# Experts of a diffusion trunk: gate and up rows alternate with single banks of the down product

## The chip, the cores and the metric

The kernel runs on one core of one Trainium2 chip. The metric is the device time of one execution in microseconds. A second figure, the span, is the time from the first to the last instruction in one profiled execution.

## The reference

One layer of a trunk over 128 context tokens and 512 latent tokens of width 2048: adaLN modulation, a mixer (12 attention heads and 32 state-space groups), an output projection, and then a routed feed-forward part with 16 experts. Only the last is touched by the change. All of it is float32.

```python
def expert_choice_ffn(x, p):
    B, L, D = x.shape
    cap = CAPACITY_FACTOR * L // N_EXPERTS
    aff = jax.nn.softmax((x @ p['w_router']).astype(jnp.float32), axis=-1)
    g, idx = lax.top_k(jnp.swapaxes(aff, 1, 2), cap)
    bidx = jnp.arange(B)[:, None, None]
    xs = x[bidx, idx]
    h = (jax.nn.silu(jnp.einsum('becd,edf->becf', xs, p['w_gate']))
         * jnp.einsum('becd,edf->becf', xs, p['w_up']))
    y = jnp.einsum('becf,efd->becd', h, p['w_down']) * g[..., None].astype(x.dtype)
    return jnp.zeros_like(x).at[bidx, idx].add(y)
```

Each expert takes 64 latent and 16 context tokens (80 slots), has gate and up matrices of 2048x1024 and a down matrix of 1024x2048, 8 MB each, and adds its result to the output rows of its tokens.

## The kernel before, in words

The program is written engine by engine, and the order of each engine's instructions is the order in the source. Semaphores tie the engines together.

**Weights.** An expert's weights come in twelve pieces of 2 MB: pieces 0 to 7 hold in turn an eighth of what the gate and up products need (even ones gate, odd ones up: four of the sixteen 128-row blocks of the contraction), pieces 8 to 11 a quarter of down (two of its eight contraction blocks). SyncE (SP) issues them in the order 0, 1, 8, 2, 3, 9, 4, 5, 10, 6, 7, 11 into a ring of 8 slots (`w_ring`, which lies in the buffers `work` and `hT_`). Before each issue it waits until `s_used` says that the piece that was in the slot before has been multiplied. The profile puts that wait of SP at line 105 and the issue at line 690.

**TensorE.** `gate_up(s, j, r, rounds)` multiplies one gate or up piece (an "eighth"): 4 contraction blocks ("rows" here, one value of k each) of 8 blocks of hidden units in 2 halves, so 64 matmuls, 16 a row. The weights of the expert are the stationary side, 128x64, and the 80 tokens the moving side; the result lies in PSUM banks 0 to 2, summed over k. `down(e, s, k, r, rounds)` multiplies one contraction block of the down matrix of the expert before (an eighth of down): three banks (3, 4, 5), in each four matmuls side by side, each in its own strip of 32 columns of the array. There the hidden values are the stationary side (128x32 or 128x16) and 512 columns of weights the moving side.

**Order.** `expert(e, s, ...)` goes through nine steps j: in step j, the 64 matmuls of gate or up piece j of expert e (j below 8), then the 12 matmuls of down block j - 1 of expert e - 1 (j above 0), and in odd steps the transposes (`turn_four`, four matmuls at line 1187) of the next expert's tokens. At its start it waits for the hidden values of expert e - 1 (`s_hh`), which ScalarE (lines 1170, 1171) and VectorE (lines 2262, 2264) form from banks 0 to 2. In step 1 each bank of down waits for VectorE (lines 2276, 2280) to have read the result of the expert before it out of that bank (`s_ye`). The down block of an odd k, like every piece of gate and up, gives its slot back with its last matmul.

Expert 0 has gate and up alone, through `gate_up`. Fifteen calls of `expert` follow (e = 1 to 15), and at the end `last_down` (line 1795) does the down product of expert 15.

Of the kernel before, what the change touches and what calls it, by code (L numbers as in the profile page):

```python
# [15 lines left out]
KT = D // P  # L16
# [24 lines left out]
BANK = 512  # L41
# [6 lines left out]
START = 12  # L48
# [35 lines left out]
def trunk_step(nc, t, out):  # L84

    ctx = ExitStack()
    with ctx:
# [8 lines left out]
        def free_sem(name, start=START):  # L96


            s = sem(name)
            free.append((s, start))  # L100
            return s
# [13 lines left out]
        def bank(b, n=BANK, at=0):  # L115
            return PS[:, b * BANK + at:b * BANK + at + n]
# [197 lines left out]
        RING = RING_SLOTS  # L314
        w_ring = [work[:, i * 4096:(i + 1) * 4096] for i in (1, 6, 2, 3, 4, 5)] + [hT_[:, 6144:6144 + 4096], work[:, 0:4096]]
# [3 lines left out]
        xsT = [hT_[:, i * 1280:(i + 1) * 1280].rearrange("p (k s) -> p k s", k=KT) for i in range(2)]  # L319
        act_g = hT_[:, 2560:2560 + 8 * SLOTS]  # L320
        actT = [hT_[:, 3200 + i * 640:3840 + i * 640].rearrange("p (k s) -> p k s", k=8) for i in range(2)]
# [128 lines left out]
        s_used = free_sem("s_used")  # L450
        s_sg = sem("s_sg")
        s_hh = free_sem("s_hh")
        s_ye = free_sem("s_ye")
# [22 lines left out]
        ORDER = [0, 1, 8, 2, 3, 9, 4, 5, 10, 6, 7, 11]  # L476
# [708 lines left out]
        def _(pe):  # L1185
# [221 lines left out]
            for g in range(6 * TT):  # L1407
                m, at_ = (g - SSM_FIRST) // SSM_EACH, (g - SSM_FIRST) % SSM_EACH
# [192 lines left out]
            for k in range(1, 7):  # L1601
                tt = (k + 2) // 3
                first = 5 * ((k + 2) % 3)
# [79 lines left out]
            for tt in range(1, 4):  # L1683
                for s in range(5):
                    i = 5 * (tt - 1) + s
# [36 lines left out]
            def turn_four(e, s, b):  # L1722

                pe.wait_ge(s_xsev, 4 * e + b)
                for k in range(4 * b, 4 * b + 4):
                    last = turn(bank(7, P, (k - 4 * b) * P), xs[s][:, k * P:(k + 1) * P])
                last.then_inc(s_xsT, 1)

            def hidden_at(u, f):

                return bank(2 * u, SLOTS, f * SLOTS) if f < 6 else bank(1, SLOTS, (2 * u + f - 6) * SLOTS)

            def landed(r, rounds):
                pe.wait_ge(s_w[r % RING], 16 * (rounds + r // RING + 1))

            def gate_up(s, j, r, rounds):


                landed(r, rounds)
                u = j % 2  # L1740
                w = w_ring[r % RING].rearrange("p (k b m i) -> p k b i m", k=4, b=4, i=2)
                for k in range(4 * (j // 2), 4 * (j // 2) + 4):
                    for f in range(8):
                        opens = k == 0 and (f == 0 or (f == 6 and u == 0))
                        for h in range(2):
                            last = pe.matmul(hidden_at(u, f)[64 * h:64 * h + 64, :],  # L1746
                                             w[:, k % 4, f // 2, f % 2, 64 * h:64 * h + 64], xsT[s][:, k, :],
                                             start=opens, stop=(k == KT - 1), skip_group_check=True)
                last.then_inc(s_used, 1)

            def down(e, s, k, r, rounds):

                if k % 2 == 0:
                    landed(r, rounds)
                w = w_ring[r % RING].rearrange("p (k n) -> p k n", k=2)
                for c in range(3):
                    if k == 0:
                        pe.wait_ge(s_ye, START + 6 * (e - 1) + 2 * c + 2)
                    for g, first, n, col in ((0, 0, 32, c), (1, 32, 32, c), (2, 64, 16, c), (3, 32 * c, 32 if c < 2 else 16, 3)):
                        last = pe.matmul(bank(3 + c)[32 * g:32 * g + n, :], actT[s][:, k, first:first + n],  # L1760
                                         w[:, k % 2, col * BANK:(col + 1) * BANK], start=(k == 0), stop=(k == 7))
                if k % 2 == 1:
                    last.then_inc(s_used, 1)

            def expert(e, s, r0, rounds, tokens):

                pe.wait_ge(s_xsev, 4 * e + 4)
                pe.wait_ge(s_hh, START + 2 * e)
                for j in range(9):
                    if j < 8:  # L1770
                        gate_up(s, j, r0 + ORDER.index(j), rounds)
                    if j:
                        down(e - 1, 1 - s, j - 1, r0 + ORDER.index(8 + (j - 1) // 2), rounds)
                    if tokens is not None and j % 2 == 1:
                        if j == 1:
                            pe.wait_ge(s_gath[1 - s], tokens)
                        turn_four(e + 1, 1 - s, j // 2)
# [5 lines left out]
            for j in range(8):  # L1783
                gate_up(0, j, j, 0)
                if j % 2 == 1:
                    if j == 1:
                        pe.wait_ge(s_gath[1], 32)
                    turn_four(1, 1, j // 2)
            for e in range(1, EXPERTS):
                expert(e, e % 2, 12 * e - 4, 0, 32 * ((e + 1) // 2 + 1) if e + 1 < EXPERTS else None)  # L1790
# [503 lines left out]
        def _(pool):  # L2294
# [145 lines left out]
            def shifted(tt, b):  # L2440
                pool.wait_ge(s_scaled, SCALED + 4 * (tt - 3) + b + 1)
                rows, (_, shift) = turned_views(tt, b, shift2)
                TT_(rows, rows, shift, ALU.add).then_inc(s_h2, 1)
# [107 lines left out]
```

## Time and profile before

| | |
|---|---|
| median of 3 runs | 2412.14 us (2411.34 to 2412.56) |
| profiled execution, its own time | 2406.91 us |
| its span | 2405.1 us |
| mean granted TensorE clock over the span | 0.982 |
| the fifteen calls of `expert` (from 1404.20 to 2363.07 us of the span) | 958.87 us |
| busy: TensorE matmul / weight load | 2249.6 us (94%) / 1477.0 us (61%) |
| busy: VectorE / ScalarE / GpSimd | 716.9 / 480.9 / 621.2 us |
| data moved | 630.85 MB |

The profile names an instruction by its line, its engine, and output <- inputs. PE is TensorE's matmul and PEld its weight load. The trace shows every float32 matmul as two records of each kind where single records are counted (the timeline): the 64 matmuls of an eighth are x128 there, the four of a bank x8; the view by lines counts them once. Ends of matmuls are modelled, so starts are better to reckon with than ends. "issue" as a releaser means that the engine waited for nothing that the profile shows. The calls of `expert` are told apart by VectorE's instruction at line 2262, which runs once an expert.

### The profile page before, as it was taken

The numbers are of one execution on the slowest core, as the hardware profiler recorded it, in microseconds if no ns is written. First come the engines' busy times: TensorE is split into PE (matmuls) and PEld (weight loads), VectorE is DVE, ScalarE is ACT, GpSimd is POOL, SyncE is SP. The second block draws the span as 40 slices with busy tenths as digits, with TensorE's granted clock in tenths as the row PEclk, the third lists the DMA queues.
The fourth block names the chain that finished last, engine by engine and source line by source line (L and its number), as shares of the span: only waits on it lengthen the run. The fifth ranks groups of instructions, "written<-read, shape, count | busy, mean of one in ns | idle before, by whom it ended". The sixth has DMA issues, their size and how long they took to land.

```text
span 2405.1 us, 57415 instructions
## 1 busy us (share of the span) xinstructions
PE 2249.6 (94%) x25897; PEld 1477.0 (61%) x25897; DVE 716.9 (30%) x1172; ACT 480.9 (20%) x1020; POOL 621.2 (26%) x660
## 2 busy tenths in 40 slices
PE   5999999999999999999996589999999999999997
PEld 3468888656566565644443476667667666666663
DVE  4124442367767775311337000000000000000001
ACT  3011111356665654210024000000000000000000
POOL 0246771466766673000205100000000000000000
PEclk9999999999999999999998799999999999999999
DMA  9922222865565654240334989999999999999995
GB/s 370 365 84 60 86 55 70 228 201 163 188 220 166 201 193 145 98 157 27 143 122 175 334 333 395 408 409 409 409 414 410 416 414 410 410 408 402 407 405 184
DMA packets 184669, 630.85 MB, mean 262 GB/s; under 512 B 14618, under 2 KB 91204, under 8 KB 154020
## 3 DMA queue, kind: packets, MB, share of 16 engines
q1 hardware_dynamic: 165920, 587.11, 63.6%
q0 software_dynamic: 3328, 20.97, 3.3%
q10 hardware_dynamic: 15188, 19.19, 2.4%
q8 instruction: 203, 3.33, 0.6%
q14 instruction: 30, 0.25, 0.0%
HBM read 602.80 MB, written 24.44 MB: 261 GB/s over the span
## 4 chain that ended last, share of the span: by engine, by line
PE 69%; DMA 14%; DVE 6%; issue 4%; SPq 2%; ACT 2%; POOL 1%; ACTq 1%; DVEq 0%; POOLq 0%
PE PS L1746 19%; PE PS L1496 11%; PE PS L1587 10%; DMA work<-in_w_gate 9%; PE PS L1760 9%; PE PS L1310 8%; DMA hT_<-in_w_gate 3%; PE PS L1252 3%; PE PS L1187 3%; POOL work L2398 1%; DVE PS L2096 1%; PE PS L1214 1%; PE PS L1482 1%; DMA work<-in_w_ada 1%; DVE work L2055 1%
## 5 line engine op out<-in xcount | busy, mean ns | idle before, releaser
L1746 PEld LDWEIGHTS PS<-hT_,work 128*64 128x64 f32 x14336 | 512.0, 140 | 91.5 <-issue 71.2
L1746 PE MATMUL PS<-hT_,work 128*64 128x80 f32 x14336 | 530.8, 235 | 34.0 <-issue 21.0
L1496 PE MATMUL PS<-hT_,work 128*128 128x512 f32 (+1 forms) x1536 | 433.2, 434 | 0.0
L2398 POOL TENSOR_TENSOR work<-work 128x512 f32<-128x512 f32 x240 | 305.1, 1271 | 163.8 <-ACT work L1002 147.8
L1496 PEld LDWEIGHTS PS<-hT_,work 128*128 128x128 f32 x1536 | 226.5, 192 | 146.8 <-issue 146.7
L1760 PE MATMUL PS<-work,hT_ 128*32 128x512 f32 (+1 forms) x2544 | 298.6, 596 | 4.6 <-DMA work<-in_w_down 3.0
L2262 DVE TENSOR_TENSOR hT_<-PS,hT_ 128x480 f32<-128x480 f32 x16 | 10.5, 658 | 947.4 <-ACT hT_ L1170 947.4
L1587 PE MATMUL PS<-work,mixT_ 128*128 128x512 f32 x640 | 283.1, 598 | 0.0
L2480 POOL DMA_INDIRECT out_y<-mixT_,work x16 | 23.4, 1461 | 797.8 <-DVE mixT_ L2280 797.8
L1310 PE MATMUL PS<-work,hT_ 128*128 128x256 f32 x960 | 212.7, 381 | 0.7 <-DMA work<-in_w_in 0.7
L1164 ACT ACTIVATE hT_<-PS 128x256 f32<-128x256 f32 x64 | 24.5, 383 | 943.9 <-PE PS L1187 943.9
L1587 PEld LDWEIGHTS PS<-work,mixT_ 128*128 128x128 f32 x640 | 120.0, 191 | 142.0 <-issue 142.0
L1310 PEld LDWEIGHTS PS<-work,hT_ 128*128 128x128 f32 x960 | 180.6, 190 | 26.1 <-issue 1.2
L1002 ACT ACTIVATE work<-work,cT 128x512 f32<-128x512 f32 x256 | 172.7, 717 | 50.4 <-POOL work L2398 38.1
L1760 PEld LDWEIGHTS PS<-work,hT_ 128*32 128x32 f32 (+1 forms) x2544 | 70.4, 105 | 146.9 <-issue 134.8
L2096 DVE SCALAR_TENSOR_TENSOR PS<-work,cT,PS 128x512 f32<-128x512 f32 x208 | 155.9, 750 | 3.5
L1187 PE MATMUL PS<-consts,mixT_ 128*128 128x128 f32 (+2 forms) x403 | 62.2, 292 | 49.0 <-DMA mixT_<-h_rows,work 25.9
L1187 PEld LDWEIGHTS PS<-consts,mixT_ 128*128 128x128 f32 (+2 forms) x403 | 45.0, 153 | 101.1 <-issue 58.5
L1746 PEld LDWEIGHTS PS<-hT_ 128*64 128x64 f32 x2048 | 72.1, 139 | 14.5 <-issue 8.2
L1746 PE MATMUL PS<-hT_ 128*64 128x80 f32 x2048 | 75.0, 234 | 5.8 <-DMA hT_<-in_w_gate 4.6
L1252 PE MATMUL PS<-work,hT_ 128*128 128x512 f32 x160 | 73.7, 612 | 0.9 <-DVE hT_ L1920 0.9
L1187 PE MATMUL PS<-consts,work 128*128 128x128 f32 (+4 forms) x361 | 53.4, 267 | 19.2 <-DVE work L2249 8.0
(301 smaller groups left out, 1848.1 us busy)
## 6 DMA issues: line engine op xcount, KB each, us to landing
work<-in_w_up SPq DMA_DIRECT2D x57, 2048.0 KB, 27.3
work<-in_w_down SPq DMA_DIRECT2D x56, 2048.0 KB, 32.2
work<-in_w_gate SPq DMA_DIRECT2D x55, 2048.0 KB, 31.7
work<-in_w_ada SPq DMA_DIRECT2D x48, 2048.0 KB, 9.6
work<-in_w_in SPq DMA_DIRECT2D x80, 512.0 KB, 6.3
hT_<-in_w_gate SPq DMA_DIRECT2D x9, 2048.0 KB, 33.9
work<-in_w_out SPq DMA_DIRECT2D x4, 4096.0 KB, 13.7
hT_<-in_w_down SPq DMA_DIRECT2D x8, 2048.0 KB, 31.2
```

Source lines behind the costliest of these rows:

```text
L1002: act.activation(prod[i % 3] if k else acc_ctx[p % 3], late_ring[k // 8][:, k % 8, :], ACT.Identity, scale=cTv[:, 0, k:k + 1]).then_inc(s_ ...
L1164: act.activation(xsT[s][:, 4 * b:4 * b + 4, 0:CAP_L], rows[:, :, 0:P:2], ACT.Copy)
L1187: return pe.transpose(dst, src, ident[0:parts, 0:parts])
L1214: last = pe.matmul(bank(5 + part)[q:q + 32, :], cT_wide[:, k, :], w_ada_ring[n % ADA_RING][:, k % 8, :], start=(k < 4), stop=(k >= KT - 4))
L1252: last = pe.matmul(bank(tt), hT[:, k, tt * P:(tt + 1) * P], w_chunk[k // 2 % NW][:, BANK * (k % 2):BANK * (k % 2) + BANK], start=(k == 0), ...
L1310: last = pe.matmul(bank(g % 2, 256), hT[:, k, tt * P:(tt + 1) * P], w_chunk[chunk % NW][:, 256 * (k % 4):256 * (k % 4) + 256], start=(k == ...
L1496: last = pe.matmul(qk_bank(which)[:, (ctx_at if ctx_ else lat_at)[which]], w_chunk[chunk % NW][:, HD * (k % 8):HD * (k % 8) + HD], hT[:, k ...
L1587: last = pe.matmul(bank(tt), mix_at(k)[:, tt * P:(tt + 1) * P], w_out_ring[n % 2][:, k, :], start=(k == 0), stop=(k == HEADS - 1 if n == 0 ...
L1746: last = pe.matmul(hidden_at(u, f)[64 * h:64 * h + 64, :], w[:, k % 4, f // 2, f % 2, 64 * h:64 * h + 64], xsT[s][:, k, :], start=opens, s ...
L1760: last = pe.matmul(bank(3 + c)[32 * g:32 * g + n, :], actT[s][:, k, first:first + n], w[:, k % 2, col * BANK:(col + 1) * BANK], start=(k = ...
L2096: ch.link(STT(acc_bank, w, c, acc_bank, ALU.mult, ALU.add))
L2398: TT_(acc_ctx[p % 3], acc_ctx[p % 3], prod[i % 3], ALU.add).then_inc(s_padd, 1)
```

## The change

The body of `gate_up` becomes a function for one row (`gate_up_row`), the body of `down` one for one bank (`down_bank`). A step of `expert` with both products now goes: row 0, row 1, bank 0, row 2, bank 1, row 3, bank 2. Before it was rows 0 to 3, then banks 0 to 2. The matmuls are the same and as many; `s_used` is raised in the same order, by the last matmul of row 3 and of bank 2. Expert 0 and `last_down` are as before. In step 0 there is no down block and in step 8 no gate or up block, so both keep their order.

```diff
+            def gate_up_row(s, j, k, r):
+
                 u = j % 2
                 w = w_ring[r % RING].rearrange("p (k b m i) -> p k b i m", k=4, b=4, i=2)
+                for f in range(8):
...
+                if k % 4 == 3:
+                    last.then_inc(s_used, 1)
...
+            def down_bank(e, s, k, c, r, rounds):
+
+                if k % 2 == 0 and c == 0:
                     landed(r, rounds)
                 w = w_ring[r % RING].rearrange("p (k n) -> p k n", k=2)
...
+                if k == 0:
+                    pe.wait_ge(s_ye, START + 6 * (e - 1) + 2 * c + 2)
+                for g, first, n, col in ((0, 0, 32, c), (1, 32, 32, c), (2, 64, 16, c), (3, 32 * c, 32 if c < 2 else 16, 3)):
+                    last = pe.matmul(bank(3 + c)[32 * g:32 * g + n, :], actT[s][:, k, first:first + n],
+                                     w[:, k % 2, col * BANK:(col + 1) * BANK], start=(k == 0), stop=(k == 7))
+                if k % 2 == 1 and c == 2:
                     last.then_inc(s_used, 1)
...
                 for j in range(9):
                     if j < 8:
-                        gate_up(s, j, r0 + ORDER.index(j), rounds)
-                    if j:
-                        down(e - 1, 1 - s, j - 1, r0 + ORDER.index(8 + (j - 1) // 2), rounds)
+                        landed(r0 + ORDER.index(j), rounds)
+                        gate_up_row(s, j, 4 * (j // 2), r0 + ORDER.index(j))
+                    for c in range(3):
+                        if j < 8:
+                            gate_up_row(s, j, 4 * (j // 2) + c + 1, r0 + ORDER.index(j))
+                        if j:
+                            down_bank(e - 1, 1 - s, j - 1, c, r0 + ORDER.index(8 + (j - 1) // 2), rounds)
```

TensorE's order in steps 2 and 3 of the first call of `expert`, before (L1746 is gate and up, L1760 is down, x64 the 64 matmuls of an eighth, L1187 the transposes):

```order
L1187 MATMUL PS<-consts,mixT_ 128x128 x4
L1746 MATMUL PS<-hT_,work 64x80 x64
L1760 MATMUL PS<-work,hT_ 32x512 x2
L1760 MATMUL PS<-work,hT_ 16x512
L1760 MATMUL PS<-work,hT_ 32x512 x3
L1760 MATMUL PS<-work,hT_ 16x512
L1760 MATMUL PS<-work,hT_ 32x512 x3
L1760 MATMUL PS<-work,hT_ 16x512 x2
L1746 MATMUL PS<-hT_,work 64x80 x64
```

and of the changed kernel in step 2, where the same lines are L1743 and L1763:

```order
L1187 MATMUL PS<-consts,mixT_ 128x128 x4
L1743 MATMUL PS<-hT_,work 64x80 x32
L1763 MATMUL PS<-work,hT_ 32x512 x2
L1763 MATMUL PS<-work,hT_ 16x512
L1763 MATMUL PS<-work,hT_ 32x512
L1743 MATMUL PS<-hT_,work 64x80 x16
L1763 MATMUL PS<-work,hT_ 32x512 x2
L1763 MATMUL PS<-work,hT_ 16x512
L1763 MATMUL PS<-work,hT_ 32x512
L1743 MATMUL PS<-hT_,work 64x80 x16
L1763 MATMUL PS<-work,hT_ 32x512 x2
L1763 MATMUL PS<-work,hT_ 16x512 x2
```

The one run of 64 stands now as 32, 16 and 16, and the twelve matmuls of down as three times four behind them.

## Rows read from the trace of the kernel before

**Rows 1.** Windows of five calls of `expert`, and the sum over all fifteen calls.
```profile
core 0: us, PE busy (x) PEld busy (x) DVE busy (x) ACT busy (x) POOL busy (x), PEclk, DMA share, GB/s
...
1466.03:1529.54 63.51, 61.17 (x1236) 43.18 (x1232) 5.39 (x8) 2.65 (x11) 3.66 (x6) 1.00 1.01 409
...
1781.74:1844.90 63.16, 61.60 (x1236) 43.47 (x1232) 5.39 (x8) 2.65 (x11) 3.64 (x6) 1.00 1.01 410
...
1909.33:1975.79 66.46, 61.79 (x1236) 43.16 (x1232) 5.39 (x8) 2.65 (x11) 3.65 (x6) 1.00 1.01 410
1975.79:2042.87 67.08, 63.60 (x1236) 44.83 (x1232) 5.39 (x9) 2.65 (x11) 3.64 (x6) 0.97 1.01 411
...
2238.06:2302.74 64.68, 61.61 (x1236) 42.97 (x1232) 5.39 (x9) 2.65 (x11) 1.64 (x2) 1.00 1.00 403
...
sum 958.87, PE 920.20 PEld 647.70 DVE 76.34 ACT 37.87 POOL 48.09; mean PE 61.35 PEld 43.18 DVE 5.09 ACT 2.52 POOL 3.21
```

**Rows 2.** TensorE's waits from 1404.20 to 2363.07: total us, times, longest.
```profile
PE PS L1746 <- issue: 17.9, 25, 3.5
PE PS L1746 <- DMA work<-in_w_gate: 10.4, 8, 2.2
PE PS L1746 <- DMA hT_<-in_w_gate: 4.6, 3, 1.7
PE PS L1760 <- issue: 3.0, 5, 1.1
PE PS L1760 <- DMA work<-in_w_down: 3.0, 4, 1.3
PE PS L1746 <- DMA work<-in_w_up: 1.8, 2, 1.2
```

**Rows 3.** SP's waits over the whole span, the longest row.
```profile
SPq L105 <- PE PS L1760: 545.4, 58, 14.0
```

**Rows 4.** DMA issues, first call of `expert` (1404.20 to 1466.03): median us to landing.
```profile
work<-in_w_gate SPq DMA_DIRECT2D x4, 2048.0 KB, 14.2
```

**Rows 5.** The same, from 1975.79 to 2042.87.
```profile
work<-in_w_gate SPq DMA_DIRECT2D x3, 2048.0 KB, 35.2
```

**Rows 6.** Timeline of TensorE's weight loads, 1817.8 to 1828.4: start, us, records.
```profile
1817.84 0.16 PEld L1760 LDWEIGHTS PS<-work,hT_ 128*32 128x32 f32 x8
...
1819.58 0.12 PEld L1760 LDWEIGHTS PS<-work,hT_ 128*16 128x16 f32 x4 [0.31 <-issue]
1820.55 4.49 PEld L1746 LDWEIGHTS PS<-hT_,work 128*64 128x64 f32 x128 [0.85 <-issue]
1825.13 0.16 PEld L1760 LDWEIGHTS PS<-work,hT_ 128*32 128x32 f32 x8
...
1827.84 0.42 PEld L1187 LDWEIGHTS PS<-consts,mixT_ 128*128 128x128 f32 x4 [0.85 <-issue]
```

**Rows 7.** Weight loads at steps 0 and 1 of one call, two eighths without down between.
```profile
1846.51 7.04 PEld L1746 LDWEIGHTS PS<-hT_,work 128*64 128x64 f32 x201 [0.85 <-issue]
```

**Rows 8.** Weight loads of two down blocks in a row, steps 7 and 8 of expert 15.
```profile
2362.29 0.16 PEld L1760 LDWEIGHTS PS<-work,hT_ 128*32 128x32 f32 x8
2362.75 0.13 PEld L1760 LDWEIGHTS PS<-work,hT_ 128*16 128x16 f32 x4 [0.30 <-issue]
...
2366.61 0.12 PEld L1760 LDWEIGHTS PS<-work,hT_ 128*16 128x16 f32 x4 [0.31 <-issue]
```

**Rows 9.** TensorE's waits from 1404.20 to 1656.
```profile
PE PS L1746 <- issue: 8.3, 8, 3.5
```

**Rows 10.** TensorE's waits from 2106.71 to 2302.74.
```profile
PE PS L1746 <- issue: 2.4, 5, 0.7
```

**Rows 11.** VectorE around the start of a call: last of the hidden values, last reading of a result.
```profile
1845.48 0.32 DVE L2264 TENSOR_TENSOR hT_<-PS,hT_ 128x160 f32<-128x160 f32 x1
...
1850.67 0.76 DVE L2280 SCALAR_TENSOR_TENSOR mixT_<-PS,work,mixT_ 16x512 f32<-16x512 f32 x1
```

More of the change, by code:

```diff
@@ L1734, in landed @@
                 pe.wait_ge(s_w[r % RING], 16 * (rounds + r // RING + 1))
+            def gate_up_row(s, j, k, r):
+                u = j % 2
+                w = w_ring[r % RING].rearrange("p (k b m i) -> p k b i m", k=4, b=4, i=2)
+                for f in range(8):
+                    opens = k == 0 and (f == 0 or (f == 6 and u == 0))
+                    for h in range(2):
+                        last = pe.matmul(hidden_at(u, f)[64 * h:64 * h + 64, :],
+                                         w[:, k % 4, f // 2, f % 2, 64 * h:64 * h + 64], xsT[s][:, k, :],
+                                         start=opens, stop=(k == KT - 1), skip_group_check=True)
+                if k % 4 == 3:
+                    last.then_inc(s_used, 1)
@@ L1736, in gate_up @@
             def gate_up(s, j, r, rounds):
                 landed(r, rounds)
-                u = j % 2
-                w = w_ring[r % RING].rearrange("p (k b m i) -> p k b i m", k=4, b=4, i=2)
                 for k in range(4 * (j // 2), 4 * (j // 2) + 4):
[L1743 to L1748, printed above, removed]
@@ L1749, in gate_up @@
-                last.then_inc(s_used, 1)
-            def down(e, s, k, r, rounds):
-                if k % 2 == 0:
+                    gate_up_row(s, j, k, r)
+            def down_bank(e, s, k, c, r, rounds):
+                if k % 2 == 0 and c == 0:
                     landed(r, rounds)
                 w = w_ring[r % RING].rearrange("p (k n) -> p k n", k=2)
[L1756 to L1762, printed above, removed]
+                if k == 0:
[4 more added lines that the diff above has]
+                if k % 2 == 1 and c == 2:
```

## The prediction

> **What bounds the kernel now.** I read the windows by call of `expert` first, since the change touches those fifteen calls and nothing else. They take 958.87 us in sum. The DMA engines are busy all the time (share 1.00 to 1.01, 403 to 411 GB/s), and TensorE is busy for 920.20 of the 958.87 us [rows 1]. So both are close to full, and the question is which one has slack. Three views answer it.
>
> TensorE's waits say that it waited for weights for 10.4 + 4.6 + 3.0 + 1.8 = 19.8 us in all fifteen calls, and for nothing that the profile shows for 17.9 + 3.0 = 20.9 us [rows 2]. SP's waits say that it nearly always stood in front of a full ring, waiting for TensorE to give a slot back [rows 3]. The landing times say how the ring was filled: in the first call a gate piece landed 14.2 us after its issue [rows 4], in the tenth after 35.2 us [rows 5]. A slot is issued again as soon as it is free, so a longer landing time means that more of the eight slots were still under way and fewer lay ready. The DMA engines thus lost ground to TensorE from call to call. The six calls from 1466.03 to 1844.90 took 378.87 / 6 = 63.1 us each, at TensorE's pace; the six from 1909.33 to 2302.74 took 393.41 / 6 = 65.6 us each, at the pace of the transfers, TensorE waiting a little for weights in them [rows 1]. So I have two prices: TensorE needs about 63.1 us for an expert as it runs, stalls without a visible cause included, and the transfers need 65.6 us where they set the pace. Work added on TensorE is free only for the first 2.5 us an expert, and only in the later calls; in the early ones it counts at once, though there it also saves the lead that the transfers would lose later.
>
> **What the change removes, adds and moves.** No matmul is added or taken away. What changes is how often TensorE goes over from 64-column tiles with 80 moving columns to 32-column tiles with 512, and back. In a step with both products, before: once there and once back. Now: three times each. That is two more pairs of changes a step, in steps 1 to 7, in fifteen calls: 2 x 7 x 15 = 210 pairs.
>
> The price of a pair comes from starts of weight loads. An eighth of gate or up between two down blocks runs from 1820.55 to 1825.13, 4.58 us for 128 records; a down block from 1825.13 to 1827.84, 2.71 us, and from 1817.84 to 1820.55 the same [rows 6]. Without a change of tiles in between: 201 records of gate and up loads took 7.04 us, of which the last record itself is some 0.14, so (7.04 - 0.14) / 200 = 34.5 ns a record, and 128 of them 4.42 us; the same reckoning on the 4.49 us of the single eighth gives 34.3 ns and 4.39 us [rows 6, 7]. That those 201 cross from one piece to the next with no gap shows that the wait for the piece, already met, costs nothing. Two down blocks in a row go on at one set of four strips every 0.43 us: from 2362.75 to 2366.61 are 9 steps, 0.429 us each, so 2.57 us a block of six [rows 8]. The pair thus costs (4.58 - 4.39) + (2.71 - 2.57) = 0.33 us. One sees where: inside a block the loads run one step ahead of the matmuls, at a change they don't. The last loads of down start at 1819.58, and the next loads only 0.97 us later instead of 2 x 0.43 [rows 6].
>
> The added path is 210 x 0.33 = 69.3 us, or 4.6 us an expert. What no row shows is a block as short as one row (32 records, 1.10 us) or one bank (0.86 us). By its loss of 0.19 and 0.14 us, I take the row at 1.29 and the bank at 1.00. The ends: nothing, if a row's loads could run under a bank's long stream; and at the top the idle time that the loads show after a down block, 0.85 us against 0.30 within one, 0.55 more, with the 0.22 on the other side (0.19, and 0.03 from the block's first load to its second step) 0.77 us a pair, 162 us [rows 6]. I take 0.33, since it is a difference of starts on the path itself, and the 0.55 holds matmuls that are running.
>
> TensorE at its own pace then needs 63.1 + 4.6 = 67.7 us an expert, above the 65.6 us of the transfers. So the transfers keep their lead for all fifteen calls, and the waits for weights go: -19.8 us. The call from 1975.79 ran at a mean granted clock of 0.97, in which one of the longest of these waits fell [rows 1, 2]; I take 2 us off for that (0.03 of 67.08). The 20.9 us without a visible cause stay in: they were 8.3 us in the first four calls, when landing times were short, and 2.4 us in three of the late ones, so they don't come from a long queue of weights [rows 9, 10].
>
> Sum: 69.3 - 19.8 - 2 = 47.5 us.
>
> Costed at nothing, with their cover:
> - The slot of a gate or up piece comes back two banks and three changes later, about 2 us. SP's issue behind it, and the down piece queued behind that, move by as much. With TensorE slower than the transfers several slots lie ready; if the transfers still set the pace, it would cost these 2 us once, when the ring first runs dry, and not each time.
> - Hidden values: TensorE goes on at 1846.51, VectorE had finished them at 1845.80 [rows 7, 11]. In step 7 the last row now ends one bank (1.00 us) before the transposes instead of 2.71 before them. The chain of ScalarE and VectorE starts behind those transposes' evacuation in the program anyway, so it isn't later; the cover is 0.7 us a call, 10 us if I am wrong on it.
> - Bank 0 of step 1 is reached two rows earlier. VectorE has read the last bank at 1851.43 [rows 11]; bank 0 would come at about 1846.51 + 4.4 + 2.2 = 1853.1. 1.7 us to spare.
>
> The profiled execution's own time is 2406.91 us, 1.8 beyond its span; the median of the runs is 5.2 us above it. 2406.91 + 47.5 = 2454.4 for that execution, 2459.6 against the median; I say 2459.
>
> **A rule against this sum.** All loads that the rows show at a change of tiles start after the last step of the block before has been streamed [rows 6]. The Trainium skill has a rule on either side. "TensorE: Matmul & The Clock Gate", the section on the mechanism of tiling, says that a weight load that goes to the background buffer is pulled ahead of matmuls in flight; taken by itself it would hide every load, and the sum would be nothing added. "TensorEngine Tiling (Array Packing)", Key Properties, says that a change of tiling mode drains the engine; by that the pairs count, at a price that the page doesn't give. Inside a block the trace agrees with the first, at a change with the second.
>
> **The rivals.**
> 1. *The stalls without a cause shrink.* With TensorE slower and the DMA engines less than full, the 20.9 us may go, if they are some fetch that is late. Then 47.5 - 20.9 = 27 us, 2439. For it: TensorE consumes instructions 7% more slowly. Against: they were most when the queue was shortest [rows 9, 10].
> 2. *Short blocks cost more.* If a row of 1.1 us doesn't get its loads into step before the next change, each pair may cost half as much again, 0.50 us: 105 - 21.8 = 83 us, 2495. For it: the idle of the loads is nearly as long as a bank. Against: a block's second step comes after 0.46 us (2362.29 to 2362.75) and every later one after 0.43, so it is in step at once [rows 8].
> 3. *Not slower: the pair is cheap and falls into the waits for weights.* The loads of a row run under the stream of the bank before, as the first rule above would have it. Below 19.8 / 210 = 0.09 us a pair, everything fits in what TensorE waits for now, and the time stays at 2410 to 2414; it can't fall much, since the transfers are full from the second call on. For it: the 19.8 us exist. Against: 0.33 us in every step of the trace.
> 4. *The change doesn't do what it says*: TensorE runs its instructions in program order here, and the order shows the split, so I give this no chance of its own.
>
> **How the numbers follow.** Forecast 72%, rival 1 13%, rival 2 7%, rival 3 6%, something on the faster side 2%. What a measurement of this kernel can tell from no change is about 0.2%, 4.8 us. Rivals 1 and 2 are slower too: slower 0.93, same 0.05, faster 0.02. The forecast's own range takes 0.30 to 0.36 us a pair (63 to 76 us) and a few us of the stalls: 2450 to 2468. The range of 8 in 10 goes most of the way to rival 1 and part of the way to rival 2: 2437 to 2478.
>
> **What would show it.** Right: in the windows by call, all at 66.5 to 68.5 us with no rise to the later ones, and a DMA share below 1; landing times of gate pieces that stay under 20 us; no waits for weights left; single rows 1.29 us and single banks 1.00 us from start to start, and an idle time of the loads near 0.85 us three times a step. Wrong: loads of a row that start 0.43 us after the last loads of a bank; calls of 63 us; or waits of TensorE for weights that stay as they were.

## The result, and the profile after

| | before | changed |
|---|---|---|
| median | 2412.56 us (2411.34 to 2415.46, 5 runs) | 2424.86 us (2422.94 to 2427.01, 5 runs) |
| ratio | | 1.0049, 95% interval 1.0035 to 1.0064 |
| again, in later rounds | 2411.42 us (15 runs) | 2423.27 us, 1.0051 (1.0037 to 1.0064) |
| profiled execution / span | 2406.91 / 2405.1 us | 2427.01 / 2425.2 us |
| fifteen calls of `expert` | 958.87 us | 975.50 us |

The change costs 12 us. It was forecast to cost 47. The direction was right, the size wrong by a factor of four, and the measured time is below the range of 2437 to 2478 us.

The windows by call come first again (us, busy time and count of PE, PEld, DVE, ACT, POOL, then granted clock, DMA share and GB/s), as [rows 1]:

```profile
1408.30:1474.13 65.83, 64.84 (x1220) 43.89 (x1224) 0.89 (x2) 2.55 (x11) 1.03 (x2) 0.97 0.86 340
...
1539.62:1604.35 64.73, 64.73 (x1236) 42.38 (x1232) 5.38 (x8) 2.65 (x11) 3.67 (x6) 1.00 1.01 405
...
1995.52:2061.28 65.76, 64.90 (x1236) 42.52 (x1232) 5.39 (x8) 2.65 (x11) 3.65 (x6) 1.00 1.00 405
...
2257.60:2322.14 64.54, 64.54 (x1236) 42.32 (x1232) 5.39 (x8) 2.65 (x11) 1.64 (x2) 1.00 1.00 404
...
sum 975.50, PE 969.05 PEld 636.77 DVE 76.32 ACT 37.87 POOL 48.09; mean PE 64.60 PEld 42.45 DVE 5.09 ACT 2.52 POOL 3.21
```

The calls are even: 64.5 to 66.4 us from first to fourteenth, where before they went from 62 to 67. In six of them TensorE is busy for every us, and in none does it wait for weights. So TensorE sets the pace throughout. The DMA share stayed at 1.00 to 1.01 from the second call to the fourteenth, though the prediction wanted it below 1; here a full share is no sign of which side sets the pace. TensorE's waits in the calls, as [rows 2]:

```profile
PE PS L1743 <- issue: 9.0, 10, 3.5
```

No wait for weights is left (19.8 us before), and the waits without a visible cause are 9.0 us instead of 20.9. A gate piece landed after 11.4 us in the first call and 21.0 us in the tenth, against 14.2 and 35.2 [rows 4, 5]; the prediction wanted under 20 throughout:

```profile
work<-in_w_gate SPq DMA_DIRECT2D x4, 2048.0 KB, 11.4
...
work<-in_w_gate SPq DMA_DIRECT2D x3, 2048.0 KB, 21.0
```

The weight loads of one step, as [rows 6]:

```profile
1823.60 2.28 PEld L1743 LDWEIGHTS PS<-hT_,work 128*64 128x64 f32 x64 [0.84 <-issue]
1825.96 0.16 PEld L1763 LDWEIGHTS PS<-work,hT_ 128*32 128x32 f32 x8
1826.96 1.17 PEld L1743 LDWEIGHTS PS<-hT_,work 128*64 128x64 f32 x32 [0.84 <-issue]
1828.22 0.16 PEld L1763 LDWEIGHTS PS<-work,hT_ 128*32 128x32 f32 x8
1829.22 1.17 PEld L1743 LDWEIGHTS PS<-hT_,work 128*64 128x64 f32 x32 [0.84 <-issue]
1830.48 0.14 PEld L1763 LDWEIGHTS PS<-work,hT_ 128*32 128x32 f32 x8
1831.46 0.42 PEld L1187 LDWEIGHTS PS<-consts,mixT_ 128*128 128x128 f32 x4 [0.84 <-issue]
```

From start to start, two rows take 2.36 us, a single row 1.26, a bank 1.00, 1.00 and 0.98. The step is 7.86 us long (1823.60 to 1831.46), against 4.58 + 2.71 = 7.29. The two added pairs of tile changes cost 0.57 us, 0.285 each, and not the 0.33 of the forecast.

### The profile page after: what moved, and what is told of

Its sections match the earlier page's. It is cut to its first block, busy times and chain, and to the rows that moved or that the text cites. A ratio compares the mean times of both kernels' runs of the same rounds, so it can differ in the third digit from the quotient of the medians.

```text
span 2425.2 us, 57415 instructions
## 1 busy us (share of the span) xinstructions
PE 2301.2 (95%) x25897; PEld 1467.6 (61%) x25897; DVE 714.8 (29%) x1172; ACT 480.9 (20%) x1020; POOL 621.1 (26%) x660
## 4 chain that ended last, share of the span: by engine, by line
PE 81%; DVE 6%; issue 4%; DMA 2%; SPq 2%; ACT 2%; POOL 1%; ACTq 1%; DVEq 0%; POOLq 0%
PE PS L1743 26%; PE PS L1763 15%; PE PS L1496 11%; PE PS L1587 9%; PE PS L1310 8%; PE PS L1187 3%; PE PS L1252 3%; POOL work L2405 1%; DVE PS L2103 1%; PE PS L1214 1%; PE PS L1482 1%; PE PS L1802 1%; DMA work<-in_w_ada 1%; DVE work L2062 1%; SPq L678 1%
## 5 line engine op out<-in xcount | busy, mean ns | idle before, releaser
L1743 PEld LDWEIGHTS PS<-hT_,work 128*64 128x64 f32 x14336 | 519.5, 139 | 219.2 <-issue 217.6
L1743 PE MATMUL PS<-hT_,work 128*64 128x80 f32 x14336 | 565.5, 236 | 13.6 <-issue 12.9
L1763 PE MATMUL PS<-work,hT_ 128*32 128x512 f32 (+1 forms) x2544 | 331.5, 601 | 0.0
L1187 PE MATMUL PS<-consts,mixT_ 128*128 128x128 f32 (+2 forms) x403 | 62.6, 293 | 49.7 <-DMA mixT_<-h_rows,work 25.8
L1187 PEld LDWEIGHTS PS<-consts,mixT_ 128*128 128x128 f32 (+2 forms) x403 | 45.5, 154 | 101.0 <-issue 58.0
L1743 PEld LDWEIGHTS PS<-hT_ 128*64 128x64 f32 x2048 | 73.9, 138 | 34.9 <-issue 34.9
L1743 PE MATMUL PS<-hT_ 128*64 128x80 f32 x2048 | 81.4, 235 | 1.5 <-issue 1.5
L1763 PEld LDWEIGHTS PS<-work,hT_ 128*32 128x32 f32 (+1 forms) x2544 | 51.7, 104 | 45.8 <-issue 21.3
L1187 PE MATMUL PS<-consts,work 128*128 128x128 f32 (+4 forms) x361 | 53.4, 267 | 19.2 <-DVE work L2256 8.0
```

Source lines behind the costliest of these rows:

```text
L1187: return pe.transpose(dst, src, ident[0:parts, 0:parts])
L1743: last = pe.matmul(hidden_at(u, f)[64 * h:64 * h + 64, :], w[:, k % 4, f // 2, f % 2, 64 * h:64 * h + 64], xsT[s][:, k, :], start=opens, s ...
```

## The experiments

Theory A: TensorE's stalls without a visible cause come where gate and up matmuls stand in long runs, and the alternation takes them away by cutting the runs. Theory B: they belong to the full transfers, and go as soon as TensorE is the slower side. Ratios are to the kernel before in the same rounds.

**1. As much time added to TensorE, without the alternation.** Four more matmuls stand at the end of each down block, in steps 1 to 7; nothing reads their result.

```diff
-            def down(e, s, k, r, rounds):
+            def down(e, s, k, r, rounds, eight=False):
...
+                    if c == 2 and not eight:
+                        for g, first, n, col in ((0, 0, 32, c), (1, 32, 32, c), (2, 64, 16, c), (3, 32 * c, 16, 3)):
+                            last = pe.matmul(bank(6, 342)[32 * g:32 * g + n, :], actT[s][:, k, first:first + n],
+                                             w[:, k % 2, col * BANK:col * BANK + 342], start=True, stop=True)
```

> The order of before, with TensorE made slower by about what the alternation costs: at the end of the down block of each step 1 to 7 four more matmuls side by side, 342 columns, into an unused PSUM bank (their result is not read). 2 x 342 columns at the 0.43 us per 512 of the down strips are 0.57 us a step, 60 us over 105 steps. Theory A (runs): TensorE's stalls without a visible cause come where gate and up matmuls stand in a long run, and the alternation took them away by cutting the runs. Then here they stay, about 20 us in the calls plus some 11 us of small ones, only the waits for weights (20 us) go, and the time is 2412 + 60 - 20 = about 2452. Theory B (traffic): the stalls go as soon as TensorE is slower than the transfers, whatever the order. Then the calls take 975 us as in the changed kernel, and the time is 2424 to 2428 with about 9 us of such stalls.

Measured: 2447.8 us, ratio 1.0148 (1.0132 to 1.0164). A step of its trace goes from 1561.45 to 1569.32, 7.87 us: the length of the changed kernel's. Weight loads, the first of a step and the first of the transposes behind it:

```profile
1561.45 4.49 PEld L1746 LDWEIGHTS PS<-hT_,work 128*64 128x64 f32 x128 [0.57 <-issue]
...
1569.32 0.42 PEld L1187 LDWEIGHTS PS<-consts,mixT_ 128*128 128x128 f32 x4 [0.57 <-issue]
```

TensorE's waits in its calls, and the sum of the calls:

```profile
PE PS L1746 <- issue: 20.4, 23, 3.5
PE PS L1760 <- issue: 2.1, 3, 1.5
```
```profile
sum 995.85, PE 975.72 PEld 669.72 DVE 76.33 ACT 37.88 POOL 48.09; mean PE 65.05 PEld 44.65 DVE 5.09 ACT 2.53 POOL 3.21
```

The waits for weights are gone, as they should be, but 22.5 us of stalls without a visible cause are there, and the time is within 5 us of theory A's 2452. Theory B falls. With a step as long as the changed kernel's, the order alone is worth about 1% (1.0148 against 1.0049 and 1.0051). One thing is not held fixed: the added matmuls are also instructions. A step has 320 matmuls and weight loads as the timeline counts them, 40.7 a us; before it was 304 in 7.29 us, 41.7 a us, and in the changed kernel 304 in 7.86 us, 38.7 a us. Experiment 2 bears on that.

**2. Half of the change.**

```diff
+                        gate_up_row(s, j, 4 * (j // 2) + 1, r0 + ORDER.index(j))
                     for c in range(3):
-                        if j < 8:
-                            gate_up_row(s, j, 4 * (j // 2) + c + 1, r0 + ORDER.index(j))
+                        if j < 8 and c == 1:
+                            gate_up_row(s, j, 4 * (j // 2) + 2, r0 + ORDER.index(j))
+                            gate_up_row(s, j, 4 * (j // 2) + 3, r0 + ORDER.index(j))
```

> Half of the change: a step goes rows 0 and 1, bank 0, rows 2 and 3, banks 1 and 2, so one more pair of tile changes instead of two. 105 pairs x 0.285 us (half of the 0.57 us a step that the changed kernel shows) are 30 us more on TensorE. If the transfers set the pace above 65 us a call, TensorE's 60.5 + 2.0 and whatever is left of its stalls fits beneath, and the time is 2410 to 2416: same. If the cost were simply per pair, 2418 (half of the 12 us). Theory A expects stalls without a visible cause between the 20.9 us of before and the 9 of after, theory B near those of before, since the transfers are full.

Measured: 2413.93 us, ratio 1.0009 (1.0000 to 1.0018), below half of the 0.49%. TensorE's waits in its calls:

```profile
PE PS L1763 <- DMA work<-in_w_down: 10.7, 8, 2.6
PE PS L1743 <- issue: 8.5, 11, 3.5
PE PS L1743 <- DMA work<-in_w_gate: 0.3, 1, 0.3
PE PS L1763 <- issue: 0.2, 1, 0.2
```

Runs of 32 matmuls already bring the stalls down to 8.7 us; runs of 16 bring nothing more. By the price of a pair its step is about 7.57 us long, with 304 instructions, 40.1 a us: nearly the rate of experiment 1, which has 22.5 us of stalls. So the length of the runs counts, beyond the mean rate. There is still 11 us of waiting for weights, so the 30 us of the added pairs were covered nearly whole by what they took away (the calls add up to 962.3 us, 3.4 more than before). That the stalls lie as low as in the full change was not what I expected of theory A (something between).

**3 and 4. The alternation in calls 1 to 8 alone, and in 9 to 15 alone.**

```diff
+                    if j < 8 and not e <= 8:          # second kernel: not e > 8
+                        for c in range(3):
+                            gate_up_row(s, j, 4 * (j // 2) + c + 1, r0 + ORDER.index(j))
                     for c in range(3):
-                        if j < 8:
+                        if j < 8 and e <= 8:          # second kernel: e > 8
```

> The alternation in calls 1 to 8 of expert alone; calls 9 to 15 in the order of before. If the transfers are the second bound: early calls take 65.1 us (before 63.1), but the transfers keep their lead, so that late calls run at TensorE's 61 to 63 us instead of 65.6: sum 8 x 65.1 + 6 x 62.8 + 60.3 = 958 us, time 2410 to 2416, same, with landing times that rise only in the late calls. If the cost is TensorE's alone and adds up, half of the change: 2418.

> The alternation in calls 9 to 15 alone. If the transfers set the pace there (65.6 us a call before), TensorE's 65.0 us fits beneath them and nothing is added: 2411 to 2416, and TensorE still waits a little for weights. If the cost adds up call by call, 2418. Together with the run on the early calls: if both are below half of the 12 us, the cost of the change is what is left when TensorE is above the transfers in all calls.

Measured: 2412.65 us, 1.0009 (1.0000 to 1.0018), and 2415.37 us, 1.0016 (1.0007 to 1.0025). Two windows of the first kernel, the eighth call (alternating) and the eleventh (not):

```profile
1868.06:1932.84 64.78, 64.62 (x1236) 42.46 (x1232) 5.39 (x9) 2.65 (x11) 3.67 (x6) 1.00 1.01 408
...
2057.74:2119.37 61.63, 61.31 (x1236) 43.22 (x1232) 5.39 (x9) 2.66 (x11) 3.65 (x6) 1.00 1.01 410
```

The lead of the transfers is passed on: a late call in the old order takes 61.6 us here, where before the six from 1909.33 on took 65.6. It lasts for three calls; the next take 65.3, 65.8 and 64.5. The two halves add up to 0.25% where the whole is 0.49%. The interval of the second just reaches half of the whole, so that one alone would not exclude a cost that adds up call by call.

**5 and 6. A quarter of the weights' traffic, in both orders.**

```diff
-                    dst = dst.rearrange("p (b n) -> p b n", b=n)
+                    dst = dst.rearrange("p (b n) -> p b n", b=n)[:, :, 0:1024]
+                    src = src[:, :, 0:1024]
                 else:
-                    src = w_down_v[:, bass.ds(e, 1), j - 8, :].rearrange("p e n -> p (e n)")
+                    src = w_down_v[:, bass.ds(e, 1), j - 8, :].rearrange("p e n -> p (e n)")[:, 0:1024]
+                    dst = dst[:, 0:1024]
```

> The order of before, each weight piece of the experts loading only its first quarter (0.5 of 2 MB; the matmuls take what lies in the slots, so the result is not the reference's). Transfers are then no bound. Theory A (long runs alone): the stalls without a visible cause stay near 20 us, calls at about 62.5 us. Theory B (traffic): they go, and with them the small ones; calls at the clean 60.5 us, 907 us in sum against 958.87, so 2360 us.

> The changed order with the same quarter loads. Calls at 64.5 us, 965 us in sum by either theory. Against the run with the order of before, the difference is the bare price of the 210 pairs: 60 us at 0.285 us a pair (0.57 us a step), 69 at the predicted 0.33. Theory A expects less, 35 to 40, because the order of before keeps its stalls.

Measured: 2342.63 and 2400.56 us. A call of the one and of the other, and the sums:

```profile
1517.08:1577.62 60.54, 60.54 (x1236) 42.75 (x1232) 5.39 (x8) 2.65 (x11) 3.66 (x6) 1.00 0.43 128
...
sum 906.69, PE 904.23 PEld 640.78 DVE 76.33 ACT 37.89 POOL 48.09; mean PE 60.28 PEld 42.72 DVE 5.09 ACT 2.53 POOL 3.21
```
```profile
1653.60:1718.14 64.54, 64.54 (x1236) 42.33 (x1232) 5.39 (x9) 2.65 (x11) 3.65 (x6) 1.00 0.40 120
...
sum 965.84, PE 964.85 PEld 634.66 DVE 76.32 ACT 37.87 POOL 48.09; mean PE 64.32 PEld 42.31 DVE 5.09 ACT 2.52 POOL 3.21
```

Without full transfers both orders run clean, call after call within 0.1 us in most. A call costs 60.54 and 64.54 us: 4.00 us for 14 pairs, 0.286 us a pair. The medians differ by 57.9 us, 0.276 for each of the 210 pairs. Theory A in its bare form, that long runs alone stall, falls: at this traffic the order of before has 5.0 us of such stalls, 3.5 of them the one at the start of the first call that every kernel here has. Long runs and traffic are both needed.

**7. 15 of 16 parts of the weights, order of before** (3840 in place of 1024 in the edit above).

> The order of before, each piece loading 15 of its 16 parts (result not the reference's). The transfers need 65.6 x 15/16 = 61.7 us or a little more a call, just below TensorE's 63.1: the waits for weights go. Theory A: the other stalls stay at about 20 us, calls near 63, sum 945, time about 2395. Theory B: if it takes only transfers that are no longer full, they go too: sum 915, time about 2370.

Measured: 2387.54 us, ratio 0.9903 (0.9871 to 0.9935); theory A said about 2395, theory B 2370. TensorE's waits:

```profile
PE PS L1748 <- issue: 16.7, 22, 3.5
PE PS L1762 <- issue: 2.3, 4, 1.0
```

None for weights, 19.0 us without a visible cause. The stalls don't need the transfers to be the slower side.

**8 and 9. Fewer tile changes, run twice.** Two eighths stand in one run, then the transposes and two down blocks; slots come back in the order of issue.

```diff
-        USED = [0, 1, 3, 2, 4, 6, 5, 7, 9, 8, 10, 11]
+        USED = [0, 1, 2, 3, 4, 5, 6, 7, 8, 9, 10, 11]
...
-                for j in range(9):
+                for j in range(1, 8, 2):
+                    gate_up(s, j - 1, r0 + ORDER.index(j - 1), rounds)
+                    gate_up(s, j, r0 + ORDER.index(j), rounds)
+                    if tokens is not None:
...
+                        turn_four(e + 1, 1 - s, j // 2)
+                    for k in (j - 1, j):
+                        down(e - 1, 1 - s, k, r0 + ORDER.index(8 + j // 2), rounds)
```

> The other way: two eighths of gate and up in one run of 128 matmuls, then two down blocks, so 4 pairs of tile changes a call instead of 7. TensorE's clean need falls by about 3 x 0.3 = 0.9 us a call. If the transfers are the bound of before, the time is no better: 2410 to 2416. Theory A expects more stalls without a visible cause than the 20.9 us, since the runs are twice as long (over 30 us), and could make it slower, to 2420; theory B about as many.

> The kernel with few tile changes (two eighths, then two down blocks) once more, since it came out at 0.9983 of before, 0.9972 to 0.9994. If the transfers bound both, 0.998 to 1.000 again; a gain above 0.3% would mean that TensorE's cheaper order counts somewhere. Its stalls without a visible cause again over 40 us.

Measured: 2404.69 us, 0.9983 (0.9972 to 0.9994), and again 2406.04 us, 0.9979 (0.9970 to 0.9988): faster than both kernels, by 5 us than the one before. Waits of the first of these runs:

```profile
PE PS L1746 <- issue: 42.4, 48, 3.5
PE PS L1746 <- DMA work<-in_w_up: 4.2, 3, 3.2
PE PS L1187 <- issue: 3.1, 3, 1.3
```

With runs of 128 matmuls the stalls without a visible cause are 46.0 us, as theory A wants, the waits for weights 6.7 us (49.0 and 0.5 us the second time). The time doesn't suffer, and the transfers are full either way (share 1.01 from the third call on). Where the 5 us come from isn't settled. In its first call the DMA share is 0.93 (0.92 the second time), in the order of before 0.87; the earlier slots would explain some 4 us of lead, but no run took that part alone.

**10. The changed kernel again, in the same rounds.**

> The changed kernel itself, on the same chip as the run beside it and in the same rounds: 1.0049 again (1.0035 to 1.0064). The one that adds the same work without the alternation came out at 1.0148; if this one were above 1.010 on another chip, the gap between the two would be in doubt.

Measured: 2423.27 us, 1.0051 (1.0037 to 1.0064). The gap to experiment 1 stands.

**11. Half of the weights' traffic, order of before** (2048 in the edit above; one run).

> The order of before with half of each weight piece loaded (result not the reference's). It tells how much traffic the stalls want: at a quarter they were gone, at 15/16 they were 19.0 us. Theory A as it stands now (long runs and transfers close to full): nearly gone, calls at 60.5 to 61 us. If they grew with traffic in proportion, about 10 us and calls at 61.5.

Measured: 2352.36 us. Stalls 5.0 us in four, calls of 60.6 us in nine of fifteen. So they don't grow in proportion: 5.0 us at a quarter and at a half, 19.0 at 15/16, 20.9 at the whole.

**12. Long runs at a quarter of the traffic** (the edits of 8 and 5 together; one run).

> The order with runs of 128 gate and up matmuls, with a quarter of each piece loaded (result not the reference's). With full loads it had 46 us of stalls without a visible cause. If long runs stall only beside full transfers, they go, all but the 3.5 us one at the start of the first call, and a call takes 60.54 less 3 pairs of 0.286 = 59.7 us. If a run of 128 is too long by itself, calls stay at 62 us.

Measured: 2326.16 us; a call and the only wait in the calls:

```profile
1508.37:1567.98 59.61, 59.61 (x1236) 43.05 (x1232) 5.39 (x9) 2.65 (x11) 3.66 (x6) 1.00 0.46 130
```
```profile
PE PS L1748 <- issue: 3.5, 1, 3.5
```

Runs of 128 matmuls and more go clean when the transfers leave room. And three pairs fewer save 60.54 - 59.61 = 0.93 us, 0.31 a pair: the price of a change of tiles, from the other side.

**Where the stalls stand, in the traces of all these runs.** Between two stalls in one call of the kernel before, TensorE runs this:

```profile
1474.89 2.98 PE L1746 MATMUL PS<-hT_,work 128*64 128x80 f32 x78 [0.81 <-issue]
1477.81 2.78 PE L1760 MATMUL PS<-hT_ 128*32 128x512 f32 x24
1480.52 0.66 PE L1187 MATMUL PS<-consts,mixT_ 128*128 128x128 f32 x4
1481.10 4.65 PE L1746 MATMUL PS<-hT_,work 128*64 128x80 f32 x128
1485.68 2.78 PE L1760 MATMUL PS<-hT_ 128*32 128x512 f32 x24
1488.40 4.58 PE L1746 MATMUL PS<-hT_,work 128*64 128x80 f32 x125
1494.50 0.36 PE L1746 MATMUL PS<-hT_,work 128*64 128x80 f32 x3 [1.53 <-issue]
```

Both stalls fall in the middle of an eighth, where the program waits for nothing. From the one to the other are 383 matmuls, as many weight loads, and two semaphore instructions that the views leave out: 768, three times 256. And 256 instructions are what one fetch of TensorE's program brings, by the rows of the pages before and of experiment 1:

```profile
q8 instruction: 203, 3.33, 0.6%
```
```profile
q8 instruction: 210, 3.44, 0.6%
```

The first has 52136 instructions of TensorE on record, 257 a packet of 16 KB; the second has 1680 instructions more and 7 packets more. Counted through from the start of the program, all 29 stalls without a visible cause in the fifteen calls before (but for the 3.5 us one) stand at the same place of 256, and so do the 9 of the changed kernel. In the 14 traces together it is 257 of 260; the three others are of 0.3 us each, all in experiment 9. None of the 17 waits for weights before ends at that place. Each of the 257 ends 1.2 to 1.7 us after a fetch has landed: the two above at 1474.89 and 1494.50, the fetches running from 1472.41 to 1473.42 and from 1492.09 to 1493.20. So TensorE waits there for the next piece of its own instructions.

Taken instruction by instruction against experiment 5, the calls before are 52.2 us longer. Of these, 33 us lie in the 72 of 256 instructions around and behind such a place (8 before it, 64 from it on), which takes in the stalls too small to be listed; the other 19 us are the waits for weights. Why so few are left with short runs can be worked out from two figures. The 64 matmuls of an eighth are 256 instructions, one whole piece, and are used up in 4.58 us. Beside full transfers fetches seldom start that close together: less than 5.5 us apart in 2 of 143 cases in the calls before, 3 of 144 in the changed kernel, 7 of 144 at 15/16 of the traffic, but 61 of 144 at a half and 58 of 144 at a quarter. A call has some 145 / 15 = 9.7 pieces, 6.6 us each before, so the fetches keep up on the mean, and a long run outpaces them. That last step is worked out from these figures; no run moved the fetches alone.

## Why the prediction was wrong

- **The bounds were read rightly.** Ring, landing times and the two prices for a call said that added work on TensorE would make it the bound in all calls, and that the 19.8 us of waits for weights would go. They went to nothing.
- **The price of a pair was too high by a seventh.** 0.33 forecast, 0.286 measured: 60.0 us instead of 69.3. The fault is on the side of gate and up. Cutting the eighth in three costs (2.36 + 1.26 + 1.26 - 4.58) / 2 = 0.15 us for each further start, not 0.19; the bank's side is (1.00 + 1.00 + 0.98 - 2.71) / 2 = 0.135, and 0.14 was forecast. The 0.19 came from a rate of 34.3 ns a record, taken from one eighth less its last record; the 201 records had said 34.5, which gives 0.16. The trace of before held the better number. Single rows and banks behave like the whole ones; rival 2 had nothing to it.
- **The step that failed is "The 20.9 us without a visible cause stay in".** They fell by 11.9 us, to 9.0, since they were waits for the next piece of TensorE's instructions, which the short runs mostly avoid. Besides, there were stalls too small to be listed. The measure is the clean calls of experiment 5: 13 of 60.54, the last of 55.17, and the first of 61.56 less its 3.54 us stall, in sum 900.2 us. Before, 958.87 - 900.2 - 19.8 - 20.9 = 18.0 us of such small stalls were in the calls, most of them in TensorE's busy time. After, experiment 6 gives 13 x 64.54 + 60.90 + 65.55 - 3.54 = 961.9 us as clean, and 975.50 - 961.9 - 9.0 = 4.6 us are left. The clue stood in [rows 1]: TensorE was busy 61 to 63.6 us in a call, though its blocks add up to some 60.5. I had taken 63.1 us as TensorE's own pace and added the pairs on top.
- **The argument for that step was a wrong alternative.** I weighed only whether the stalls come from a long queue of weights, found that they don't [rows 9, 10], and kept them. Rival 1 ("some fetch that is late") named the right kind of cause, and the forecast gave it 13%; its time of 2439 is still 14 us too high, for the price of the pairs and the small stalls. Its reason, a slower TensorE, is not enough: experiment 1 has a step as long and keeps them. What matters most is how many gate and up matmuls stand in a row: 46 us of visible stalls at 128, 20.9 at 64, 8.7 at 32, 9.0 with 32 and 16, all beside full transfers.

The books, for the calls: +60.0 for the pairs, -19.8 waits for weights, -11.9 stalls, -13.4 small ones, makes 14.9 us. The windows show 16.6, of which 1.7 is that VectorE's mark stands later within a step, since the last row now has one bank behind it and not three (the last calls of experiments 5 and 6 differ by 5.73 us instead of 4.00). The profiled executions differ by 20.1 us; another 4.1 lie ahead of the first mark (1408.30 against 1404.20), mostly in the unchanged part, and the medians, at 12.3 us, don't show them. Forecast 47.5 - 9.3 - 11.9 - 13.4, and + 2 for the clock that I had set off apart, is the same 14.9. (The forecast and rivals 1 and 2 add up to 0.92; the prediction gives 0.93 for slower.)

By the Trainium skill, "TensorEngine Tiling (Array Packing)", Key Properties, a change of tiling mode drains TensorE. The trace agrees: the loads stand idle for 0.84 us at each of the three changes of a step, and this case puts 0.286 us on a pair.

## What to carry to other kernels

When TensorE and the transfers are both close to full, compare each call with the sum of its blocks; what is over is stalls, whether a row names them or not, and a new order can remove much of it. Where stalls have no visible cause, count the instructions from one to the next: a fixed number says that they belong to the instruction stream, and not to the data. Price a change of tile shape by starts of a block among its like and among others, and a stall by whether it moves when its surroundings are kept and one thing is changed. A cost that is covered in either half of a loop may still show in the whole, since the halves share one lead.

## What the runs showed of the hardware

TensorE's instructions come in pieces of 16 KB, 256 instructions each, and TensorE can run dry at the end of one. Nearly all of it comes where a long run of small matmuls (64 of 128x64 by 80 columns and more, one piece in 4.58 us) stands beside transfers at 390 GB/s and more. But for the 3.5 us stall below, the order of before has 1.5 us of such stalls in fifteen calls at 128 and at 230 GB/s and 15.5 at 400 GB/s; beside full transfers it has 17.4, the changed order 5.5. A stall ends 1.2 to 1.7 us after the piece has landed. What holds a fetch back beside full transfers, the DMA engines or the memory, no run here tells, and none moved the ends of the pieces while all else was kept.

The 3.5 us stall at the start of the first call is in every kernel, at any traffic. It stands at another place of the 256 than the others, the same one in all kernels, and its cause is open.
